# A two-model transformer block on one core: compression weights stored without their zero blocks, and the first FFN begun input tile by input tile

## The reference, cut to what matters

```python
for l in range(DEPTH):                      # 2
    mod = silu(c) @ w_ada[l] + b_ada[l]     # 9 rows of 1024: shift, scale, gate for each of 3 parts
    sh1, sc1, g1, sh2, sc2, g2, sh3, sc3, g3 = jnp.split(mod, 9, axis=-1)
    u = rms_norm(x) * (1 + sc1) + sh1
    x = x + 0.5 * g1 * ((silu(u @ w_gate) * (u @ w_up)) @ w_down)     # D_FF = 2816
    x = x + g2 * token_mix(rms_norm(x) * (1 + sc2) + sh2, ...)
    ...

def compress(k, w1, w2, pe):       # in token_mix, once for keys and once for values, 2 groups each
    # 31 blocks of 32 consecutive tokens, one every 16 tokens, 64 features a token
    blocks = (blocks + pe).reshape(B, G, 31, 32 * 64)
    return gelu(blocks @ w1) @ w2  # w1 is 2048 x 64, the same for both groups
```

## Time and profile before

| | us |
|---|---|
| median of three runs | 3607.72 |
| lowest and highest | 3607.11, 3608.80 |
| the profiled execution | 3609.13 |
| its span (first to last instruction) | 3607.6 |
| PE busy | 3456.9 |
| DVE, ACT, POOL busy | 1801.2, 1238.8, 294.7 |

### The profile page before, as it was taken

How to read it: one execution, slowest core, us unless ns; L and a number is a source line. 1 busy time by engine, 2 the same in 40 slices (tenths; PEclk the granted TensorE clock), 3 DMA queues, 4 the chain that set the end, 5 groups by cost and what they waited for, 6 DMA issues and landing times.

```text
span 3607.6 us, 40374 instructions
## 1 busy us (share of the span) xinstructions
PE 3456.9 (96%) x16390; PEld 2780.6 (77%) x16390; DVE 1801.2 (50%) x3126; ACT 1238.8 (34%) x2064; POOL 294.7 (8%) x242
## 2 busy tenths in 40 slices
PE   5999998999999999998999999999999999999999
PEld 4888786687888878887757878887778777878887
DVE  6665427744565743333575443334352665355433
ACT  3222326733322232223475232224322344224322
POOL 0000212002000200010210020003011000120000
PEclk9999999999999999999999999999999999999999
DMA  6565331033565622323201322322212123132332
GB/s 222 187 223 175 101 104 52 13 94 97 171 225 188 216 87 88 105 88 126 71 9 53 108 82 86 107 83 91 81 59 73 53 94 104 47 99 78 98 106 76
DMA packets 121175, 380.52 MB, mean 105 GB/s; under 512 B 13344, under 2 KB 28064, under 8 KB 120992
## 3 DMA queue, kind: packets, MB, share of 16 engines
q1 hardware_dynamic: 120992, 377.95, 31.7%
HBM read 375.80 MB, written 2.10 MB: 105 GB/s over the span
## 4 chain that ended last, share of the span: by engine, by line
PE 89%; DVE 6%; ACT 4%; POOL 1%; issue 1%; DMA 1%; SPq 0%; POOLq 0%; ACTq 0%; DVEq 0%
PE ps L428 26%; PE ps L429 25%; PE ps L430 25%; PE ps L608 2%; PE ps L517 2%; PE ps L627 1%; PE ps L462 1%; PE ps L478 1%; PE ps L464 1%; PE ps L463 1%; PE ps L471 1%; DVE s_wl L1367 1%; DMA s_raw<-w 1%; DVE s_raw L1376 1%; ACT s_wh L886 1%
## 5 line engine op out<-in xcount | busy, mean ns | idle before, releaser
L1367 DVE TENSOR_TENSOR s_wl<-s_raw,s_wh 128x1024 fp32r<-128x1024 f32 (+3 forms) x645 | 709.2, 1101 | 901.6 <-ACT s_wh L886 899.1
L428 PE MATMUL ps<-s_uh,s_wh 128*128 128x512 f32 x2760 | 1101.5, 399 | 45.8 <-DVE s_ul L1401 29.6
L429 PE MATMUL ps<-s_uh,s_wl 128*128 128x512 f32 x2760 | 1086.6, 394 | 0.0
L430 PE MATMUL ps<-s_ul,s_wh 128*128 128x512 f32 x2760 | 1085.3, 393 | 0.0
L886 ACT ACTIVATE s_wh<-s_raw 128x1024 fp32r<-128x1024 f32 (+3 forms) x645 | 587.9, 913 | 759.5 <-PE ps L430 568.4
L428 PEld LDWEIGHTS ps<-s_uh,s_wh 128*128 128x128 f32 x2760 | 525.9, 191 | 167.7 <-issue 34.6
L429 PEld LDWEIGHTS ps<-s_uh,s_wl 128*128 128x128 f32 x2760 | 526.0, 191 | 111.1 <-issue 2.7
L430 PEld LDWEIGHTS ps<-s_ul,s_wh 128*128 128x128 f32 x2760 | 525.2, 190 | 111.8
L430 PE MATMUL ps<-s_fl,s_wh 128*128 128x512 f32 x960 | 378.2, 394 | 0.0
L428 PE MATMUL ps<-s_fh,s_wh 128*128 128x512 f32 x960 | 378.2, 394 | 0.0
L429 PE MATMUL ps<-s_fh,s_wl 128*128 128x512 f32 x960 | 378.2, 394 | 0.0
(11 more groups left out here) (394 smaller groups left out, 3564.2 us busy)
## 6 DMA issues: line engine op xcount, KB each, us to landing
s_raw<-w SPq DMA_DIRECT2D x624, 512.0 KB, 3.6
s_raw<-w SPq DMA_DIRECT2D x96, 192.0 KB, 2.4
s_raw<-w SPq DMA_DIRECT2D x64, 256.0 KB, 2.6
s_raw<-w SPq DMA_DIRECT2D x19, 128.0 KB, 2.0
s_x<-x SPq DMA_DIRECT2D x1, 2048.0 KB, 10.2
out<-s_x SPq DMA_DIRECT2D x8, 256.0 KB, 2.2
s_raw<-w SPq DMA_DIRECT2D x4, 420.0 KB, 4.2
s_crow<-crow SPq DMA_DIRECT2D x2, 512.0 KB, 3.5
```

The source lines that it names most:

```text
L428: TE.matmul(o, w_hi(i, k), h, start=first, stop=False)
L429: TE.matmul(o, w_lo(i, k), h, start=False, stop=False)
L430: return TE.matmul(o, w_hi(i, k), l, start=False, stop=last)
L1367: V.tensor_tensor(wl[w][:, 0:n], raw[t % NRAW][:, 0:n], wh[w][:, 0:n].bitcast(F32), SUB).then_inc(*s_lo.up(("lo", t)))
```

## The change

Three things are changed.

1. **The start.** x comes in four transfers of two input tiles, before the constants; of these `sel` comes much later. ACT squares the even tiles and DVE the odd ones and adds them two by two, into a new buffer `fsq`; PE sums four pieces, all into one bank, and DVE adds the sums with one reduction. POOL's additions are gone. Of the modulation columns only one is made before the norm.
2. **The first FFN.** The host writes a matrix `gu10`: gate and up columns 0 to 511, side by side. Its tile k is input tile k for eight output tiles (gate 0 to 3, up 0 to 3). The stream is scale column, shift column, `gu10` tile, eight times. PE does all eight output tiles for input tile k (24 matmuls) before it goes to k + 1, in all eight banks at once. Since the norm's row lies in one of these banks, ACT copies it to SBUF (`more`) after the first tile, and DVE reads it there. DVE makes two columns, the product, the weight tile's rest and the activation's rest for each k.
3. **The compression.** The host writes `w1` without the zeros, the same 64 rows on both halves: two tiles for keys and two for values. Each matmul becomes two, one for each group, on 64 rows and with 64 moving columns; group 0 and 1 write to different banks, and the Gelu is four instructions on 64 columns.

The diff, cut to its core (plan, transfers and host side are told above):

```diff
@@ tensor_engine
+            if first:
+                four = [(x_, st, j) for j in range(4) for x_ in "gu"]
+                os = []
+                for k in range(8):
+                    for g_ in (1, 0):
+                        tiles.get("ada0", 8 * g_ + k, 0)
+                    i = get("gu10", k, 0)
+                    pe.wait_ge(*s_dve["u", st, k])
+                    for n, f in enumerate(four):
+                        c = 4 * (n % 2) + n // 2
+                        if k == 0:
+                            os.append(take(f))
+                        h, lo = wh[slot[i]][:, sl(c)], wl[slot[i]][:, sl(c)]
+                        TE.matmul(os[n][:], h, uh[:, k, :], start=k == 0, stop=False)
+                        TE.matmul(os[n][:], lo, uh[:, k, :], start=False, stop=False)
+                        ins = TE.matmul(os[n][:], h, ul[:, k, :], start=False, stop=k == 7)
...
-            o = take(("c1", st))
-            for j8 in range(4):
-                t = [get(f"c1{n}{l}", 0, j8 * 1024) for n in "kv"]
-                for jj in range(8):
-                    j = 8 * j8 + jj
+            o = [take(("c1", st, g)) for g in range(2)]
+            for j16 in range(2):
+                t = [get(f"c1{n}{l}", 0, j16 * 1024) for n in "kv"]
+                for jj in range(16):
+                    j = 16 * j16 + jj
                     for i in range(2):
...
-                        ins = TE.matmul(o[32 * i:32 * i + 31, 0:128], src, raw[t[i] % NRAW][:, sl(jj)], start=j == 0, stop=j == 31)
+                        for g in range(2):
+                            gs = slice(64 * g, 64 * g + 64)
+                            ins = TE.matmul(o[g][32 * i:32 * i + 31, 0:64], src[gs], raw[t[i] % NRAW][gs, 64 * jj:64 * jj + 64], start=j == 0, stop=j == 31)
@@ scalar_engine
-        SC.activation(acc[:], x[:, 0, :], ACT.Square).then_inc(*s_act.up(("sq0", 0)))
-        for k in range(1, 8):
-            if k > 4:
-                act.wait_ge(*s_pool["sq0", k - 4])
-            SC.activation(tmp[(k - 1) % 4][:], x[:, k, :], ACT.Square).then_inc(*s_act.up(("sq0", k), ("tail", "f10", k)))
+        for k in range(0, 8, 2):
+            act.wait_ge(*s_x_at(k))
+            SC.activation(uf(k), x[:, k, :], ACT.Square).then_inc(*s_act.up(("sq0", k)))
@@ vector_engine
-        for k in range(7):
-            ada("f10", 0, 1, k)
-            ada("f10", 0, 0, k)
-        norm("f10", 4, tmp[3])
+        for k in range(1, 8, 2):
+            dve.wait_ge(*s_x_at(k))
+            V.tensor_tensor(uf(k), x[:, k, :], x[:, k, :], MUL).then_inc(*s_dve.up(("sq0", k)))
+            dve.wait_ge(*s_dve.now())
+            dve.wait_ge(*s_act["sq0", k - 1])
+            V.tensor_tensor(uf(k), uf(k), uf(k - 1), ADD).then_inc(*s_dve.up(("sq0 pair", k // 2)))
+        ada("f10", 0, 1, 0, 0)
```

More of the change, by code:

```diff
@@ L32, in ffn @@
             for j in range(a, a + n):
+                if ahead and j < 4:
+                    continue
                 if j == 0 and u:
-                    if not ahead:
-                        pair(g, 0, u, 0)
+                    pair(g, 0, u, 0)
                 elif j < 2 and not u:
@@ L62, in plan @@
             fm(f"inA{l}", 8, c)
-        for c in range(4):
+        for c in range(2):
             for x in "kv":
@@ L273, in program @@
     with ExitStack() as c:
+        fsq = sb(c, "fsq", [128, 8, 512])
+    with ExitStack() as c:
         oA, oB = sb(c, "oA", [128, 4, 512]), sb(c, "oB", [128, 4, 512])
@@ L837, in second @@
             ring[:] = [list(range(8)), 0]
[L839 to L842, removed]
         pe.wait_ge(*CONST)
-        norm("f10", [(tmp[2], s_act["tail", "f10", 7]), (tmp[1], s_act["tail", "f10", 6]), (tmp[0], s_act["tail", "f10", 5]),
-                     (acc, s_pool["sq", "f10"])], tmp[3])
+        o = take(("ms", "f10", 0))
+        for k in range(4):
+            pe.wait_ge(*s_dve["sq0 pair", k])
+            ins = sums(o, 4 * k, uf(2 * k + 1))
+        ins.then_inc(*s_pe.up(("ps", ("ms", "f10", 0))))
+        row(("r", "f10"), tmp[3])
         for l in range(2):
@@ L848, in tensor_engine @@
                 norm("f11", tail("f11"), tmp[2])
-            ffn(f"f1{l}", None if l else first)
+            ffn(f"f1{l}", l == 0)
             norm(f"m{l}", tail(f"m{l}"), tmp[2])
@@ L939, in ffn @@
                     s = tmp[jj % 4]
[L940 to L943, removed]
+                    if jj == 0 and not first:
+                        fm_pair(g, 0, u or g, 0 if u else 1)
+                    elif (u or jj > 1) and not (first and jj < 4):
                         fm(g, 8, jj, 0, st)
@@ L948, in ffn @@
                     SC.activation(s[:], bank(("g", st, jj))[:], ACT.Silu if u else ACT.Relu).then_inc(*s_act.up(("gate", st, jj), frees=("g", st, jj)))
-                    if u and jj:
+                    if u and jj and not (first and jj < 4):
                         fm(u, 8, jj, 0, st)
@@ L1428, in apply @@
                     dve.wait_ge(*s_pe["ps", g])
-                    V.tensor_tensor(tmp[k % 4][:], src[:, k, :], bank(g)[:], MUL).then_inc(
-                        *s_dve.up(("ap", st, k), frees=g if k == n - 1 else None))
-                if k > 0:
+                    if after_k and k:
+                        dve.wait_ge(*s_act["row", st])
+                    V.tensor_tensor(tmp[k % 4][:], src[:, k, :], more[:] if after_k and k else bank(g)[:], MUL).then_inc(
+                        *s_dve.up(("ap", st, k), frees=g if k == (0 if after_k else n - 1) else None))
+                    if after_k:
+                        after_k(k)
+                        low(dst_l[:, k, :], tmp[k % 4][:], dst_h[:, k, :], s_act["uh", st, k], (*key, k))
+                elif after_k:
+                    continue
+                if k > 0 and not after_k:
                     low(dst_l[:, k - 1, :], tmp[(k - 1) % 4][:], dst_h[:, k - 1, :], s_act["uh", st, k - 1], (*key, k - 1))
@@ L1964, in second, with split @@
             barrier("s")
-        get("g10", 0, 0)
-        get("u10", 0, 0)
-        for k in range(7):
-            ada("f10", 0, 1, k)
-            ada("f10", 0, 0, k)
-        norm("f10", 4, tmp[3])
-        def later(k):
-            if k == 7:
-                ada("f10", 0, 1, 7)
-                ada("f10", 0, 0, 7, 1)
+        for k in range(1, 8, 2):
[5 more added lines that the diff above has]
+        ada("f10", 0, 1, 0, 0)
+        dve.wait_ge(*s_pe["ps", ("ms", "f10", 0)])
+        V.reduce_sum(small[:, 0:4], bank(("ms", "f10", 0))[:, 0:16].rearrange("p (k b) -> p b k", b=4), AX.X).then_inc(
+            *s_dve.up(("sum", "f10"), frees=("ms", "f10", 0)))
+        dve.wait_ge(*s_dve.now())
+        V.tensor_scalar(small[:, 0:4], small[:, 0:4], 1.0 / DM, 1e-6, MUL, ADD).then_inc(*s_dve.up(("mean", "f10")))
+        dve.wait_ge(*s_pool["rstd", "f10"])
+        diag(("r", "f10"), tmp[3], 32)
+        def later(k):
+            if k:
+                ada("f10", 0, 1, k, 0)
+            ada("f10", 0, 0, k, 0)
+        def split(k):
+            get("gu10", k, 0, 0 if k < 7 else AHEAD)
         for l in range(2):
```

90 lines of the change are left out of this document (50 added, 40 removed).

## The result

| | before | changed |
|---|---|---|
| median of the runs, us | 3608.26 (4) | 3567.34 (4) |
| lowest and highest | 3607.11, 3610.27 | 3562.72, 3571.10 |
| the profiled execution | 3609.13 | 3571.10 |
| its span | 3607.6 | 3569.3 |

The ratio is 0.9884 (95% interval 0.987 to 0.9899): 41 us faster, where 37.4 were forecast. The changed kernel was run in two more sets, further down; all its 12 runs have a median of 3564.7.

What follows compares the result with a forecast made beforehand. PE bounds the kernel, busy 3456.9 of 3607.6 us. Start 26.2 plus compression 11.2 gives 37.4 us, smaller things 0; from the median 3607.72 that forecasts 3570.3 us (forecast case 3566 to 3576), range 3560 to 3583.

Steps and rivals of the forecast that it cites:

- The start: Kernel start through 192 gate and up matmuls: the 193rd comes at 72.1 us instead of 98.3, gaining 26.2 us.
- tile 0: First FFN's first input tile: starts cold, 14 matmuls at 0.43 us, the other 10 take 2.3; PE ends at 33.9 us.
- DVE's columns at 1.39 us: First FFN: DVE makes two modulation columns per input tile, 1.39 us each, within a step of 5.77 us.
- rival 3: DVE sets the start: a column costs 2.2 us, a step 7.4; +10.7 us, 3581.0; chance 0.09.
- rival 4: Clock stays at 1.2 GHz through the 192 matmuls at the start: +36.0 us, 3606.3; chance 0.03.
- The subtraction of the weights: First FFN, DVE: 1.25 us, placed in the 1.6 us free between the product's end and the activation's subtraction.
- The price of a compression record: Compression matmuls: 27 ns a record, taken from L810; 6.9 us a layer, gain 5.6 a layer, 11.2 for two.
- rival 1: Compression faster: four tiles side by side, 64 columns in half the time, 3.4 us a layer; 7.0 less, 3563.3; chance 0.18.
- The rule that was weighed: Compression: matmuls never start closer than about 25 ns, so no layer under 6.4 us and the 3.4 us case falls away.
- No wait for HBM at the compression: Compression: four tiles and the next projection's fill five places, all landed before; 3.2 us of waiting in layer 0 vanishes.
- Gelu hidden above 3 us: After the compression: Gelu ready 7.0 us after its first half, hidden behind projection 0 when the compression takes over 3 us.
- one of the signs that I had named as wrong: A Gelu that PE waits for, after the compression; listed among things that would show the prediction wrong.

Runs made afterwards that it cites:

- split: Compression in two halves of 128 records, after the seventh and eighth inA projections, against the kernel with squares added further on DVE (8 small sum matmuls): 3564.69 us, ratio 0.9874.
- comp_wide: Changed kernel with each compression matmul moving 128 columns and not 64 (15 of 16 token places); 27 ns a record, one of two runs at 3573.30 and 3565.40 us.
- the two halves measured apart: Against the kernel before: start and first FFN changes alone, 3582.10 us, 26.3 less; compression change alone, 3592.14 us, 16.3 less.

## Why the prediction was right, point by point

- **The start, 26.2 forecast, 27.0 in the trace, 26.3 in the times.** Each mark came out within 1 us: constants 11.2 (11.3 forecast), sums 7.0 (7.0), first matmul 25.30 (25.5), 193rd 71.32 (72.1). The step that was off is tile 0: 7.4 us and not 8.4, as the clock rose at 29.2, after 3.9 us of matmuls and not 6.1 as in rows 5. Elsewhere it rose later: in split 5.9 us after the first matmul, so that the 24th starts 8.1 us after the first, here 7.1. That PE and DVE run level to the end, with no lead left, is the 0.29 us at the last tile.
- **DVE's columns at 1.39 us** held; rival 3 (2.2) and rival 4 (the clock low through the quad) didn't occur. The subtraction of the weights is hidden as argued.
- **The price of a compression record was the term that was mis-sized.** I took 27 ns, "the same pattern of tiles, and nothing in the trace goes faster", 6.9 us a layer; measured 15 ns, 3.9 us, rival 1 with its 18%. The wrong step was to carry over the time per record from L810 although the moving columns were half. With the stall in layer 1 the two layers took 3.88 and 5.62 us. comp_wide, with L810's 128 columns, takes 6.94 us: the price was exact for what it was the price of. The rows would have told: L538 and L810, with two and four tiles, agree in 106 and 107 ns for 128 columns in one tile, a time that belongs to the tile and its columns.
- **The rule that was weighed.** The Trainium skill, TensorE: Matmul & The Clock Gate, section "Wait — 56ns, not 53.3ns?", says that matmuls start no closer than about 25 ns. Counted by records, that gave an estimate of 6.4 us at least. Measured are 256 records in 3.95 us, 15 ns apart: as I used it, it is refuted. Each instruction stands as two records, so the mean is 31 ns an instruction, and that alone would not contradict it. But in comp_wide the records start in rounds of four, 6 to 7 ns apart, one round every 109 ns. Four records are at least two instructions, which thus start 14 ns apart or less: on different tiles of the array the trace does not agree with the rule.
- **No wait for HBM at the compression**: held, none in a trace with the new tiles. **Gelu hidden above 3 us**: nearly. PE waits 0.43 us for it in layer 0 (3.88 us), one of the signs that I had named as wrong. The tile ahead of it on ACT took 4.4 us to land and not 3.6.

```profile
456.81 0.24 PE L577 MATMUL ps<-s_cst,s_mq 64*128 64x64 f32 x1 [0.43 <-ACT s_mq L1039]
```

- **Not foreseen:** the stall beside instruction transfers (1.4 us in layer 1), and the 8 us by which two executions of one kernel differ through the clock. The first took something from the gain that rival 1 would have had. The second is a likely reason why the four runs beside the prediction stand 2.6 us over the median of all twelve: the recorded mean clock is 0.975 and 0.976 in the two slowest of the four (3571.10 and 3568.42), 0.978 and 0.979 in the others. Only the slowest of them has a trace.
- **The sum.** 42.6 us by the marks of the trace, 42.6 by the two halves measured apart, against 37.4 forecast; 4.4 of the 5.2 between them is the compression's price, 0.8 the start. By these marks the median should have been 3607.72 - 42.6 = 3565.1, just outside the 3566 to 3576 that I called the forecast; all twelve runs have 3564.7. That the four runs came to 3567.34, inside it, is in part luck: the price was too high, and a stall and slow executions that I did not foresee made up for part of it. The start is right by its mechanism. Of the compression, the waits that would vanish are right, and the price is not.

## What to carry to other kernels

Small fp32 matmuls on parts of the array are priced by tile. Count the moving columns that each tile gets, and let tiles with other rows or other columns take turns. A time per record taken from another line holds only at the same columns and the same number of tiles. Where the first layer waits for a chain of small steps, give PE all PSUM banks of work for the first input tile that is ready, and put the vector engine's long jobs into the waits of that chain. Once a burst runs at 15 ns a record, look for idle time marked "issue" and for a packet on the instruction queue beside it.

## What the hardware showed unexpectedly

- A record on 64 rows and 31 columns of weights with 64 moving fp32 columns costs 15 ns when four tiles take turns, 28 with two; with 128 columns and four tiles 27. Each tile is taken by a record every 56 ns with 64 columns and every 109 ns with 128.
- PE seems to run out of instructions: in nine of 16 bursts of 256 records, which take 3.9 us without a stall, it stood still for 0.9 to 1.4 us, and went on 2.2 to 2.8 us after a packet on the instruction queue had started. These were just the bursts in which such a packet started 1.0 to 1.7 us after the burst.
- The clock was granted at the lower level for 27.3 us while PE was busy without a break, in one execution, and not in the two other traces of the same kernel; it cost some 8 us against before and 11 against the second trace.
